# The second block's expert stream: one spare chunk waits for the row stores instead of for the first gather

## The reference, cut to what matters

```python
def hierarchical_moe(h, w_group, b_group, w_router, b_router, w_gate, w_up, w_down):
    tok = h.reshape(T, D)
    g_sel = argmax(tok @ w_group + b_group)                 # one of 4 groups
    e_logits = (tok @ w_router[g] + b_router)[g_sel]        # 8 experts of that group
    top_l, top_i = lax.top_k(e_logits, 2)
    weight = p_group[:, None] * softmax(top_l)
    # the tokens of every expert are gathered, then for each expert e:
    xb = tok[rows_tok]
    y = (silu(xb @ w_gate[e]) * (xb @ w_up[e])) @ w_down[e]
    out[row_tok] += y * rows_w
# and around it
x = x + hierarchical_moe(rmsnorm(x, norm2_g), ...)
return rmsnorm(x, final_g)
```

## Time and profile before

| | |
|---|---|
| median of 3 runs | 1613.4 us (1612.98 to 1616.02) |
| profiled execution, its own time | 1613.54 us |
| its span, first to last instruction | 1611.8 us |
| PE busy | 1515.4 us, 94% of the span |
| DVE, ACT, POOL busy | 41%, 32%, 29% |
| moved by DMA | 306.12 MB, 290.56 MB of it on SP's queue |
| the mixture, from the end of the logits to the end | about 1127 to 1611.8 us |

### The profile page before, as it was taken

The page is one execution under the profiler, slowest core; times in us unless marked ns, Lnnn a source line. Parts: engine busy times, 40 slices in busy tenths (PEclk is TensorE's granted clock), DMA queues, the critical chain, the costliest instruction groups (busy, mean ns, idle before and its releaser), DMA issues.

```text
span 1611.8 us, 18914 instructions
## 1 busy us (share of the span) xinstructions
PE 1515.4 (94%) x7408; PEld 1010.8 (63%) x7409; DVE 663.2 (41%) x1092; ACT 513.2 (32%) x913; POOL 474.8 (29%) x250
## 2 busy tenths in 40 slices
PE   7999999999999999999998999899699999999996
PEld 6974667887778888878866766457334343333443
DVE  3155565223643333322135679573523233232234
ACT  5236566222543333322246332424111111101112
POOL 4441114444534444444424363432100000000000
PEclk9999999999999999999999999999799999999999
DMA  7333001222232323222323222217999999999995
GB/s 300 108 101 91 2 1 38 94 92 92 77 119 95 102 92 104 92 91 92 100 74 114 98 78 66 105 52 287 350 402 427 429 429 431 430 430 425 427 426 233
DMA packets 46696, 306.12 MB, mean 190 GB/s; under 512 B 6496, under 2 KB 6624, under 8 KB 32400
## 3 DMA queue, kind: packets, MB, share of 16 engines
q1 hardware_dynamic: 41680, 290.56, 46.6%
q0 software_dynamic: 4352, 12.25, 2.1%
q10 hardware_dynamic: 576, 2.10, 0.4%
HBM read 302.84 MB, written 4.19 MB: 190 GB/s over the span
## 4 chain that ended last, share of the span: by engine, by line
PE 75%; DMA 10%; DVE 9%; ACT 3%; issue 2%; POOL 0%; SPq 0%; DVEq 0%; ACTq 0%; POOLq 0%
PE banks L407 26%; PE banks L1087 11%; PE banks L437 10%; DMA ring<-experts 8%; PE banks L1118 4%; PE banks L2219 3%; PE banks L942 2%; PE banks L417 2%; PE banks L2148 2%; PE banks L1127 2%; PE banks L2164 2%; DMA arena<-experts 1%; PE banks L799 1%; PE banks L2131 1%; PE banks L800 1%
## 5 line engine op out<-in xcount | busy, mean ns | idle before, releaser
L370 POOL TENSOR_TENSOR arena_r<-ring,arena_r 128x1024 fp32r<-128x1024 f32 x143 | 352.5, 2470 | 449.9 <-ACT arena_r L355 449.8
L407 PE MATMUL banks<-hT_r,arena_r 128*128 128x512 f32 x1216 | 389.6, 391 | 5.2 <-POOL arena_r L370 3.0
L355 ACT ACTIVATE arena_r<-ring 128x1024 fp32r<-128x1024 f32 x143 | 150.7, 1059 | 467.1 <-PE banks L407 305.9
L407 PE MATMUL banks<-arena_r 128*128 128x512 f32 x800 | 293.3, 391 | 0.0
L407 PEld LDWEIGHTS banks<-hT_r,arena_r 128*128 128x128 f32 x1216 | 228.7, 188 | 59.8 <-issue 9.2
L1087 PE MATMUL banks<-ring,arena 128*64 128x512 f32 x720 | 224.8, 611 | 14.7 <-DMA ring<-experts 13.1
L437 PE MATMUL banks<-arena_r 128*128 128x512 f32 x784 | 187.8, 394 | 2.2 <-POOL arena_r L370 1.8
L407 PEld LDWEIGHTS banks<-arena_r 128*128 128x128 f32 x800 | 150.5, 188 | 32.8
L437 PEld LDWEIGHTS banks<-arena_r 128*128 128x128 f32 x784 | 147.3, 188 | 37.2 <-POOL arena_r L370 3.5
L1087 PEld LDWEIGHTS banks<-ring,arena 128*64 128x64 f32 x720 | 72.0, 141 | 151.7 <-issue 151.7
L1707 DVE TENSOR_TENSOR resid<-resid,banks 128x1024 f32<-128x1024 f32 x63 | 74.1, 1218 | 129.2 <-PE banks L1127 129.2
(11 more groups left out here) (443 smaller groups left out, 1902.2 us busy)
## 6 DMA issues: line engine op xcount, KB each, us to landing
arena<-experts SPq DMA_DIRECT2D x42, 2048.0 KB, 15.8
ring<-stream SPq DMA_DIRECT2D x162, 512.0 KB, 3.7
ring<-experts SPq DMA_DIRECT2D x37, 2048.0 KB, 16.3
ring<-experts SPq DMA_DIRECT2D x16, 1024.0 KB, 14.9
arena<-experts SPq DMA_DIRECT2D x12, 1024.0 KB, 17.9
resid<-x ACTq DMA_DIRECT2D x4, 512.0 KB, 5.6
grow<-grows POOLq DMA_DIRECT2D x4, 512.0 KB, 6.9
rows<-arena POOLq DMA_DIRECT2D x4, 512.0 KB, 10.7
```

What stands on the lines that cost most here:

```text
L355: nc.scalar.activation(parts(name, m)[:, 0, :], tile(tile_n), ACT.Copy).then_inc(S["w_high"], 1)
L370: nc.gpsimd.tensor_tensor(w[:, 1, :], tile(tile_n), plain(w[:, 0, :]), ALU.subtract).then_inc(S["w_low"], 1)
L407: last = nc.tensor.matmul(pb[:, bank, :], w[:, a, k * P:(k + 1) * P], b[:, k, :], start=(k == 0 and part == 0), stop=(k == ND - 1 and part ...
```

## The change

In `expert_stream` the load of spare chunk 2 is moved ahead of three waits and gets a wait of its own: for the landing of the four row stores, `rows_st` at 16 x 4. The waits for `lg_done`, `norm_xn` and `xg_in` now stand ahead of spare chunk 3 alone. No instruction of another engine is changed; the lines below are moved down by one.

```diff
@@ -722,10 +722,11 @@
             spare_in(0)
             sp.wait_ge(S["sel_ready"], 1)
             spare_in(1)
+            sp.wait_ge(S["rows_st"], 16 * NT)
+            spare_in(2)
             sp.wait_ge(S["lg_done"], 1)
             sp.wait_ge(S["norm_xn"], 4 * NT)
             sp.wait_ge(S["xg_in"], 16)
-            spare_in(2)
             spare_in(3)
```

## The result

| | before | after |
|---|---|---|
| median of 12 runs each | 1613.39 us | 1616.26 us |
| ratio of the two | | 1.0022 (95% interval 1.0012 to 1.0032) |
| profiled execution, its own time | 1613.54 us | 1619.14 us |
| its span | 1611.8 us | 1617.4 us |

The kernel is 2.9 us slower, just on the edge of what can be told from no change; both interval ends are above 1. The profiled execution of the changed kernel was its second longest of 12, so its total is not compared; what is used are its single steps and the times between them.

What follows compares the result with a forecast made beforehand. PE was taken to bound the kernel up to 1194 us, bytes at 427 GB/s after; + 2.8 (later gather) - 0.9 (old chunk's rest) + 0 (SP, clock) = + 1.9 us on 1613.54, giving 1615.4, range 1612.4 to 1618.4.

Steps and rivals of the forecast that it cites:

- The bound: Whole path: first gather, then PE through pairs 0 and 1 into pair 2 up to 1194 us, then bytes at 427 GB/s.
- Steps 1 and 2: SP's queue: spare chunk 2 issued at 1138.6 instead of 1146.6, filling the DMA hole from 1142 with 4.9 us of work.
- Step 3: Behind 1150 us: the 4.9 us sent early are worth nothing, except 0.9 us from an older chunk's rest at the restart.
- Step 4: First gather beside spare chunk 2: lands 2.8 us later, bounds 0 and 6.0 us.
- Rival B: First gather served as slowly as beside a full queue: price 6.0 us, less 0.9, giving 1618.6; chance 0.15.
- rule of turns: DMA engines alternate between queues packet by packet, so 2.8 us is the most the first gather loses.
- Step 5: From gather to PE: the whole 2.8 us delay reaches pair 0's start and the 1194.3 issue; clock about 1 us, taken as 0.
- The sum: Whole kernel: + 2.8 (gather) - 0.9 (old chunk's rest) + 0 (SP, clock) = + 1.9 us, 1615.4; chance 0.58.
- A: First gather not delayed; only the 0.9 us gain is left, say 1612.6; chance 0.14.
- C: Bytes count from 1150, not 1194, so 4.9 us come off, less the gather's 2.8: 1611.4; chance 0.09.
- D: Row stores land at 1142 or later, SP passes both waits together, the change does nothing: 1613.5; chance 0.04.

Runs made afterwards that it cites:

- moved load: Kernel before with chunk 0 of pair 3 issued right behind chunk 1 of pair 2: -2.8 us, ratio 0.9983; a second time -3.8 us, 0.9975.
- half chunk: Kernel before with 1 MB of spare chunk 2 sent ahead of the first gather and pair 3's chunk 0 issued early: +0.6 us, ratio 1.0002.
- second profile: Profile of a second set of 12 runs of the changed kernel, unaltered: +4.5 us against before, ratio 1.0024.
- e4_late_gather: Kernel before with four more clears on POOL, so the first gather starts some 4 us later without traffic: +4.2 us, ratio 1.0028.
- e6_both_changes: Changed kernel with chunk 0 of pair 3 also issued early, behind chunk 1 of pair 2: +1.0 us against before, ratio 1.0009.

## Why the prediction was right, and where its sizes were off

**The bound.** Right: PE up to the restart of the queue, bytes from there. The length of 440.9 to 443.0 us in all kernels without the moved load, whatever was sent early, left out or delayed, shows it, and the moved load is the only edit that shortened it clearly, to 438.9 to 439.6 in three of its four profiles (441.7 with the half chunk).

**Steps 1 and 2.** Spare chunk 2 went out at 1141.04, not 1138.6, since the last row store took 12.8 instead of 10.6 us; in the second profile it was 1138.51. The hole was full in the first and filled to a share of 0.82 in the second (1142 to 1148), and the gather hardly differed (8.28 and 8.86).

**Step 3, worth of the bytes.** Right in the main: nothing. The 0.9 us taken off for the rest of an older chunk did not show. The restart's first load took 10.0 us in the first profile and 10.3 in the second, against 10.3 before and 9.9 in `e4_late_gather`, which changes no load; and with the 2 MB left out the older chunk was as much in front as before. The prediction had the 4.9 us make the queue run dry earlier at its end. A good part of them was idle long before, in the two holes ahead of 1162, and with the load left out ahead of 1157. The prediction had named the second wait ("pair 1's halves are too") without counting the idle DMA time in it.

**Step 4, the gather.** The gather is late because chunk 2 is beside it, as forecast; its size was 3.9 us and not 2.8 (4.5 in the second profile). The bound "no more than the chunk and the gather together need" is what failed. It gives 1144.27 + 4.9 + 0.8 = 1150.0 with the landing of spare chunk 1 in the profile after, and the gather landed at 1150.72; in the second profile spare chunk 1 landed at 1141.80, which gives 1147.5, and the gather at 1149.48. The sum took it that the engines are never idle until both are done. But the gather starts late (4.5 us behind its issue) and is then left over with the engines mostly idle (share 0.24 from 1148 to 1152). Rival B's condition, that the gather's own latency grows beside traffic, is thus in part what happened, at a lower price than its 6.0 us, since the chunk ran out. The prediction's rule of turns, by which 2.8 us was the most, did not hold as a bound, and the turns did not decide here: with packets of a quarter the gather took the same.

**Step 5.** Right: 1.97 and 1.45 us unchanged, and the start moved by the gather's delay. The clock's part was small: the issue of pair 2's chunk 2 was 3.90 us late against 4.17 for the product's start.

**The sum.** Pair 0 starts 4.2 us late (3.9 by the gather, 0.25 already there at its issue), and the last landing is 3.7 us late by the profile, against the forecast's 1.9 and medians of +2.9 and +4.5. The time was inside the range, and in the direction of the sum. That the first median, 1616.3, lies within 1 us of the forecast's 1615.4 is partly luck: the terms of the profile give about twice the forecast's loss, and the second median, 1618.2, is nearer to B's 1618.6. Against the bound of 0.2%, the first set lies at 0.22% and 2.9 us, on the line between "the same" (0.64) and slower (0.29). Two slips of the working change nothing: 0.10 and 0.13 make 0.23 and not 0.24, and a gather later by 2 to 4 us with the clock's 1 us spans 1613.6 to 1617.6, not 1613.9 to 1617.2.

**The rivals.** A (gather undisturbed) fell with 8.28 us. B's price of 6.0 us was not reached, with 3.9 and 4.5. C (bytes from 1150) fell with the load left out. D (the stores so late that SP gets past both waits together) could not have come about as written: POOL waits for the same landing of the stores before it issues the gather, so late stores hold back both. In `e6_both_changes` the last store landed at 1140.68; chunk 2 went out at 1140.70, the gather 1.0 us behind it at 1141.68, and the gather still took 7.89 us.

## What to carry to other kernels

A wait in a transfer queue may be there for the sake of another queue: before it is loosened, look at what small transfer on the path runs beside it, and price that transfer by its nearest busy row rather than by its bytes. Idle transfer time is worth something only if the queue stays full from there to the end; so find the last dry spell first, and look for a transfer whose home is already free and that only stands late in the order. Here one such line brought 2.8 and 3.8 us in two sets of runs, while the loosened wait, which sent a load 6 to 8 us earlier, cost 3 to 4.5.

## What the runs showed of the hardware

- A gather of 0.36 MB takes 4.4 to 4.5 us alone (four kernels), 5.2 and 5.3 with 1 MB of one chunk beside it, 7.9 to 8.9 with 2 MB and 9.0 with 4 MB. The step lies between 1 and 2 MB, and not in the size of the other queue's packets (8.5 us with 4 KB packets).
- On idle engines more than half of its bytes had moved 2.8 us behind the issue (0.20 MB by 1145), and its first packet came after 1.8 us. Beside 2 or 4 MB the first came after 4.3 to 4.7 us, beside 1 MB after 1.8 and 2.8.
- Of PE's waits for weights in the kernel before, one of 2.57 us (up to 1344.45) was followed by a product at a granted clock of 1.00 (1344.4 to 1348), and one of 2.07 us (up to 1430.54) by one of 8.80 us, at 0.59 in the mean (1430.5 to 1434). Which of the two follows could not be told there from the length of the wait.
- The last row store, 0.5 MB and the same work in all, took 10.4 to 14.7 us in the profiles, and the moment of the first gather's issue moved between 1140.4 and 1144.3 us (the late gather's kernel left out). Differences under 2 us are thus read from lengths between two events of one profile, not from times since its start.
